# Each fp32r product of 512 columns issued as two of 256 columns with the same stationary operand

## What is computed

```
mod = SiLU(cond) @ w_ada[l] + b_ada[l]        -> shift, scale, gate
h   = RMSNorm(x) * (1 + scale) + shift
p   = h @ w_in[l]                             (2048 x 5120)
o   = silu(gates) * branches(p)               (2048 wide)
x   = x + gate * RMSNorm(o @ w_out[l])        (2048 x 2048)
```

## Time and profile before

| | |
|---|---|
| median of the runs | 1113.76 us |
| profiled execution, first to last instruction (span) | 1113.0 us |
| mean granted clock of PE | 0.995 of full speed (2.4 GHz) |
| PE busy | 1091.5 us, 98%, 5356 matmuls |
| PEld busy | 879.1 us, 79%, 5356 loads |
| DVE busy | 705.0 us, 63% |
| ACT busy | 427.3 us, 38% |
| transfers | 242.28 MB, mean 218 GB/s |

### The profile page before, as it was taken

One profiled execution on the slowest core, in us unless ns is written; L12 is line 12 of the kernel. 1 busy time (PEld: TensorE's weight loads), 2 busy tenths in 40 slices (PEclk: granted clock), 3 DMA queues, 4 the chain that ended last, 5 costly groups with the idle time before them and its releaser, 6 DMA issues.

```text
span 1113.0 us, 13620 instructions
## 1 busy us (share of the span) xinstructions
PE 1091.5 (98%) x5356; PEld 879.1 (79%) x5356; DVE 705.0 (63%) x1029; ACT 427.3 (38%) x693; POOL 33.4 (3%) x66
## 2 busy tenths in 40 slices
PE   6999999999999999999999999999999999999997
PEld 5576687887878878888888788888888888888885
DVE  4555575767677787699966645487665766343335
ACT  4333334433636432243346852223423223243332
POOL 1000010000000000000010000000000000000000
PEclk8999999999999999999999999999999999999999
DMA  9998866454545567567884235345644554433423
GB/s 381 407 394 337 339 242 250 166 228 162 216 193 214 211 272 303 228 236 295 315 325 153 83 145 188 135 170 190 211 172 184 210 206 159 183 133 132 155 72 114
DMA packets 39327, 242.28 MB, mean 218 GB/s; under 512 B 4784, under 2 KB 4896, under 8 KB 13408
## 3 DMA queue, kind: packets, MB, share of 16 engines
q1 hardware_dynamic: 29232, 190.85, 44.8%
q0 software_dynamic: 7344, 46.29, 11.5%
q10 hardware_dynamic: 2688, 4.26, 1.4%
HBM read 237.67 MB, written 3.72 MB: 217 GB/s over the span
## 4 chain that ended last, share of the span: by engine, by line
PE 95%; DVE 2%; ACT 1%; DMA 1%; issue 1%; DVEq 0%; ACTq 0%; SPq 0%
PE bank L966 27%; PE bank L968 26%; PE bank L967 26%; PE bank L1030 3%; PE bank L1112 2%; PE bank L1051 1%; PE bank L1176 1%; PE bank L1128 1%; PE bank L1091 1%; PE bank L1135 1%; DMA x_t<-in_x_turned 1%; PE bank L917 1%; PE bank L915 1%; PE bank L916 1%; PE bank L1101 0%
## 5 line engine op out<-in xcount | busy, mean ns | idle before, releaser
L966 PE MATMUL bank<-w_hi,h_op 128*128 128x512 f32 x1114 | 450.0, 404 | 2.6 <-DVE h_op L1761 2.2
L968 PE MATMUL bank<-w_hi,h_op 128*128 128x512 f32 x1114 | 435.4, 391 | 0.0
L967 PE MATMUL bank<-w_lo,h_op 128*128 128x512 f32 x1114 | 434.5, 390 | 0.0
L1509 DVE TENSOR_TENSOR w_lo<-raw,w_hi 128x1024 fp32r<-128x1024 f32 x200 | 244.3, 1222 | 191.3 <-ACT w_hi L1221 190.9
L1221 ACT ACTIVATE w_hi<-raw 128x1024 fp32r<-128x1024 f32 x200 | 210.0, 1056 | 227.3 <-PE bank L968 211.8
L966 PEld LDWEIGHTS bank<-w_hi,h_op 128*128 128x128 f32 x1114 | 209.4, 188 | 58.0 <-issue 15.6
L968 PEld LDWEIGHTS bank<-w_hi,h_op 128*128 128x128 f32 x1114 | 209.1, 188 | 45.2
L967 PEld LDWEIGHTS bank<-w_lo,h_op 128*128 128x128 f32 x1114 | 209.6, 188 | 39.5
L966 PE MATMUL bank<-w_hi,o_low 128*128 128x512 f32 x192 | 75.8, 395 | 0.0
L968 PE MATMUL bank<-w_hi,o_low 128*128 128x512 f32 x192 | 74.9, 390 | 0.0
L967 PE MATMUL bank<-w_lo,o_low 128*128 128x512 f32 x192 | 74.8, 390 | 0.0
(11 more groups left out here) (227 smaller groups left out, 929.8 us busy)
## 6 DMA issues: line engine op xcount, KB each, us to landing
raw<-in_w_in SPq DMA_DIRECT2D x68, 1024.0 KB, 5.3
dot_raw<-in_ada_tiles POOLq DMA_DIRECT2D x32, 1024.0 KB, 5.1
raw<-in_w_out SPq DMA_DIRECT2D x32, 1024.0 KB, 4.9
raw_first<-in_ada_first SPq DMA_DIRECT2D x21, 1024.0 KB, 11.1
raw<-in_ada_groups SPq DMA_DIRECT2D x16, 1024.0 KB, 6.7
raw<-in_ada_halves SPq DMA_DIRECT2D x16, 1024.0 KB, 4.7
open_raw<-in_w_in SPq DMA_DIRECT2D x24, 512.0 KB, 11.5
dot_raw<-in_ada_first SPq DMA_DIRECT2D x11, 1024.0 KB, 10.1
```

Source lines behind the costliest of these rows:

```text
L966: pe.matmul(out, operand(layer, kind, 0, k, t), hi, start=k == begin, stop=False)
L967: pe.matmul(out, operand(layer, kind, 0, k, t), lo, start=False, stop=False)
L968: last = pe.matmul(out, operand(layer, kind, 1, k, t), hi, start=False, stop=k == end)
L1509: dve.tensor_tensor(w_lo[:, half % WRING, :, :].rearrange("p k n -> p (k n)"), src, hi, ALU.subtract)\
```

## The change

A helper `product` takes the place of each `pe.matmul` with 512 columns in the three functions. It issues two matmuls: columns 0 to 255 of the moving operand into columns 0 to 255 of the bank, and then columns 256 to 511 into the other half of the same bank, both with the same stationary operand. `start`, which clears the bank's marks at the beginning of an accumulation, is given with the first half alone. What is signalled to others is signalled by the second half. Order, operands, waits and all other engines stay. The built program has 9388 matmuls in place of 5356 (4032 more), and 9388 loads of a stationary operand in place of 5356: each matmul has its own load, the second half's too.

```diff
+HALF_CW = CW // 2
...
+            def product(out, stationary, moving, start, stop):
+
+                for a in range(0, CW, HALF_CW):
+                    last = pe.matmul(out[:, a:a + HALF_CW], stationary, moving[:, a:a + HALF_CW],
+                                     start=start and a == 0, stop=stop, skip_group_check=True)
+                return last
...
-                    pe.matmul(out, operand(layer, kind, 0, k, t), hi, start=k == begin, stop=False)
-                    pe.matmul(out, operand(layer, kind, 0, k, t), lo, start=False, stop=False)
-                    last = pe.matmul(out, operand(layer, kind, 1, k, t), hi, start=False,
+                    product(out, operand(layer, kind, 0, k, t), hi, start=k == begin, stop=False)
+                    product(out, operand(layer, kind, 0, k, t), lo, start=False, stop=False)
+                    last = product(out, operand(layer, kind, 1, k, t), hi, start=False,
                                      stop=k == end)
```

More of the change, by code:

```diff
@@ L914, in tile_steps @@
                     lo = w_lo[:, half % WRING, k % 2, :]
-                    pe.matmul(out, operand(layer, kind, 0, k, t), hi, start=False, stop=False)
-                    pe.matmul(out, operand(layer, kind, 0, k, t), lo, start=False, stop=False)
-                    last = pe.matmul(out, operand(layer, kind, 1, k, t), hi, start=False, stop=k == KT - 1)
+                    product(out, operand(layer, kind, 0, k, t), hi, start=False, stop=False)
+                    product(out, operand(layer, kind, 0, k, t), lo, start=False, stop=False)
+                    last = product(out, operand(layer, kind, 1, k, t), hi, start=False, stop=k == KT - 1)
                     if t == FINAL and k % 2:
@@ L980, in late_tile @@
                     lo = w_lo[:, half % WRING, k, :]
-                    pe.matmul(out, operand(1, "uc", 0, k, FINAL), hi, start=k == 0, stop=False)
-                    pe.matmul(out, operand(1, "uc", 0, k, FINAL), lo, start=False, stop=False)
-                    last = pe.matmul(out, operand(1, "uc", 1, k, FINAL), hi, start=False, stop=False)
+                    product(out, operand(1, "uc", 0, k, FINAL), hi, start=k == 0, stop=False)
+                    product(out, operand(1, "uc", 0, k, FINAL), lo, start=False, stop=False)
+                    last = product(out, operand(1, "uc", 1, k, FINAL), hi, start=False, stop=False)
                 last.then_inc(mm_done, 1)
```

## The result

The changed kernel takes 1157.4 us (median of 2 runs, 1157.27 and 1157.54) against 1113.76 before: 1.039 times as long, 95% interval 1.037 to 1.041. That is 43.6 us more, where 53.8 were forecast (1168 us). It lies in the range of 1113 to 1218 and in the likeliest case's own, 1151 to 1191.

What follows compares the result with a forecast made beforehand. PE issuing its list was taken as the bound. 4032 products at 13.3 ns more add 53.8 us to the 1113.0 us span, giving 1166.8, plus 0.8 to the median: 1168 us predicted, range 1113 to 1218.

Steps and rivals of the forecast that it cites:

- the likeliest case: Halves 118 to 122 ns apart, plus 0 to 7 us behind side products: 1151 to 1191 us, given 54%.
- 1, the distance of halves: 512-column products: 13.3 ns surcharge paid once each, so halves 120.0 ns apart, two 240.0; adds 53.8 us over 4032 products.
- 2, the second load: Same stationary operand loaded again for the second half; hidden in the 120.0 ns, 8 ns short of the bound: nothing added.
- 3, behind side products: First products behind transposes cost some 5 ns more each; price taken as staying: nothing added, up to 7 us for the range.
- 4, instructions: 8064 more entries nearly double PE's list; fetching and issue keep up: nothing added.
- 5, waits: PE's waits: none added, and early ones absorb next to none of the growth; the tail moves as a block.
- From span to time: Whole kernel: the median of the runs lies 0.8 us above its span, turning 1166.8 us into 1167.6.
- A: Rival on the 512-column products: surcharge goes with columns, 113 to 115 ns a half, 1113.8 to 1127 us; 18%.
- B: Rival on the 512-column products: the 13.3 ns vanish, load floor rules, 224 ns a product, 1103 us; 6%.
- C: Rival on the halves: load becomes the bound with surcharge behind it, 250.7 ns a product, 1211 to 1218 us; 14%.
- D: Rival on the halves: short pass falls to float32 rate, 216 ns a half, 1942 us, or anything above 1220; 6%.
- E: Rival on the split: second load dropped or halves run as one, 227 to 230 ns a product, 1103 to 1127 us; 2%.

Runs made afterwards that it cites:

- The quarters: Four matmuls of 128 columns in place of each 512-column product, where the changed kernel has two of 256; 1987.98 us in one run.

## Why the prediction was right, by its steps

- **What bounds the kernel: right.** The kernel still ends when PE has issued its list, and the time moved with the distance of PE's starts.
- **1, the distance of halves: right to the nanosecond,** 120.0 forecast and read. The reason given was in part right. Three widths with one surcharge show that it is paid once a matmul (384 columns: 173.3, not 170.0). That it is a load's share of the stream was only argued: one run speaks for it (64 stationary columns in halves: 113.3) and one against (in whole products: 230.0), and dense bfloat16 operands had almost none of it with the same 128 columns to load. So the number rests on the right count, once a matmul, and not on a known mechanism.
- **2, the second load: right.** It is made, and 112 ns are hidden under 120. The quarters show the floor, 111 to 112 ns. A half's 106.7 ns of columns alone would not cover it; of the surcharge 5 ns are needed for that.
- **3, behind side products: the term that was mis-sized.** It was taken as staying, with up to 7 us more. It went from +4.2 to -1.0 us, a gain of 5.2. Whole products are out of step for some eight matmuls behind other work; halves are not. This is half of the 10 us by which 53.8 was too much.
- **4, instructions: right.** 31 packets more, and PE's waits on "issue" round to 0% of the chain.
- **5, waits: right for the products.** The 1.7 us for `raw_first` are ahead of them. That the start of the kernel can differ by 3 us between two executions was not foreseen; it goes with PE's clock there and not with the edit.
- **From span to time: 1.0 us too little.** The 0.8 us added to the span should have been 1.8, as all executions show. It did no harm, since the span of 1113.0 that it was added to was 1.0 us above that of a usual execution.
- **The rivals.** A (by column) fell with 384 columns, B (the floor alone) with the 120.0, C with the quarters, D with the 120.0 too, E with 9388 loads. B would have given 224 ns a product and a slightly faster kernel.

The sum for the two profiled executions then reads 53.8 - 5.2 - 3.2 - 2.9 = 42.5 us of span. The medians are 1.1 us further apart, because the profiled execution of the kernel before was about 1 us longer than its median. Of the 10.2 us between 53.8 and the 43.6 measured, 5.2 are explained by term 3; the 3.2 at the side work and the rest were not taken apart by an experiment.

## What to carry to other kernels

Before cutting a matmul into pieces, read three distances between starts from the trace: that of the stream as it is, what it has on top of its columns, and that of loads with almost nothing to stream. With the float32r operands here, a piece cost its columns plus the full surcharge, and never less than a load (112 ns), and the same stationary operand was loaded for each piece. And compare the distance with the bare streaming time: the gain found here was in how the operand is stored and read, not in the shape, and it was bought with fewer bits. Last, set a time beside the span of the same execution, and look at the granted clock before a difference at the start of a kernel is put down to an edit.

## What the runs showed of the hardware that I had not expected

- Float32r products of 512 columns stood 226.7 ns apart or, on the mean, 230 to 232 ns. The second was read behind side work, beside products of another width and with smaller loads: 64 stationary columns cost 7 to 8 us instead of gaining 9 to 25.
- The surcharge of a one-cycle pass was 13.3 ns with float32r operands, 12 ns (512 columns) and 6.7 ns (256) with bfloat16 read with gaps, and 2 to 3 ns with dense bfloat16. A step of 4 bytes a column may be the common cause of the first two. No run separates the stationary operand's step from the moving one's, and it stays open.
- A long stream does not lend its spare time to the load that comes after the next: 384 + 128 columns took 287 ns, 256 + 256 took 240.
- The same start of the kernel took 22.3 to 22.6 us at 2.4 GHz, and 24.0 to 26.0 us where the granted clock was at 1.2 GHz for 3.4 to 10.2 us of it. The kernel before ended only about 1 us later by it.
